# A GpSimd hand in the second output projection: who makes one weight remainder of fourteen

## The chip, the cores and the metric

The kernel runs on one core of a Trainium2 chip. The metric is the device time of one execution in microseconds (us), the median over several runs. The core has five engines that run side by side, each through its own list of instructions in order: TensorE (PE in the profile) multiplies matrices, VectorE (DVE) and ScalarE (ACT) and GpSimd (POOL) work element by element, SyncE (SP) issues DMA transfers. They wait for each other only at semaphores, which count up and are waited for as "at least n".

## The reference, cut to what matters

```python
def first_block(x, ...):
    for layer in range(2):
        y = retention or latent attention of x        # (512, 2048) gated, times w_out (2048, 1024)
        x = _layer_norm(DEEPNORM_ALPHA * x + y, ln_g[layer], ln_b[layer])
...
def _mla_layer(...):
    ...
    return (o * jax.nn.silu(gate)) @ w_out            # the second output projection
...
h = rmsnorm(x, norm_mix_g)                            # second_block begins with it
```

All arrays are float32. 512 tokens, width 1024. The change concerns the product `(o * silu(gate)) @ w_out` of the second layer: (512 x 2048) by (2048 x 1024).

## The kernel before, in words

**Split operands.** A float32 operand is used as two parts: `hi` is a copy that is rounded to the type fp32r (ScalarE makes it), `lo` is what the rounding took away, operand minus `hi` (called the remainder; VectorE or GpSimd makes it with one subtraction, whose two inputs both lie in SBUF). A product takes three matmuls, hi x hi, lo x hi and hi x lo (lines 614 to 616).

**Seven products.** The three output projections AO, BO and DN save an eighth of the multiplications with seven block products in place of eight. In BO each block product `f` (0 to 6) takes two weight panels, so the stage runs over 14 panels, `d` from 0 to 13. A panel is 128 x 2048 floats and goes through five hands:

- SP loads it into one of three stages (`seven_load`, L672); the load of panel `d` waits until the remainder of panel `d - 3` is made, since it lands in the same stage (semaphore `d_tlo`, which counts two halves of every panel).
- ACT rounds the operand (`operand_hi`, semaphore `d_shi`), but only when PE has done the product of panel `d - 3` (`d_pe`), and then the two halves of the panel (`weights_hi`, semaphore `d_thi`). Both are instructions of line 1616.
- DVE makes the operand's remainder (`operand_lo`), the two halves of the panel's remainder (`remainders`, both on L2286) and between the halves the operand of the next panel (`combine`, L2299 to L2305).
- PE multiplies: 24 matmuls a panel, `seven(BO, d, (0, 1))`; the first half of the panel is needed at its first matmul, the second at its thirteenth.
- DVE also adds finished block products into the residual `xres` (`gathers(BO, 1, d)`, lines 2345 to 2378), ahead of `remainders(BO, d)`.

GpSimd makes the remainder of panel 0 (`weights_lo(BO, 0)`) and then has nothing to do until the input weights of the next layer (`split_lo(L0 + 2)`, L793).

**Behind the stage** VectorE goes straight on to the layer norm and the RMS norm of four token tiles (`norms`, lines 2444 to 2471), whose results PE transposes (L996) and multiplies by the next weights. The first instruction of it, L2444, waits for the product of panel 11.

The order on each engine is the order in which the code is written; nothing reorders it. Tile names: `br_hi`, `br_lo`, `s_hi`, `s_lo` are the operand parts (three in turn), `whi`, `wlo`, `whi_a`, `wlo_a` the panel parts, `bT` the input, `comb` combined inputs, `bx` kept block products.

Of the kernel before, what the change touches and what calls it, by code (L numbers as in the profile page):

```python
# [76 lines left out]
BO = Seven(2, 14, 14, END + 8, 8, (36, 36, 36, 36), ((2, 3), (4, 5), (6, 7), (0, 1), (2, 3), (4, 5), (6, 7)))  # L77
UPN, UA = 16, 28
DN = Seven(4, UA + 2 * UPN, 28, END + 16, 16, (36, 36, 36, 40), ((0, 1), (2, 3), (4, 5), (6, 7), (0, 1), (2, 3), (4, 5)))
PANELS = DN.w + 16  # L80
GATHERS, COPIES = 16, 4
HALF = SEQ // 2


# [51 lines left out]
def program(nc, t, out):  # L136
    with ExitStack() as ctx:
        def sb(name, shape, dt=F32, where=ctx):
            return where.enter_context(nc.sbuf_tensor(name, shape, dt))

        def gap(name, lines, where=ctx):
            if lines:
                sb(name, [P, 16 * lines], F32, where)

        def sem(name):
            return ctx.enter_context(nc.semaphore(name))
# [17 lines left out]
        with ExitStack() as h:  # L164
            vs_a = sb("vs_a", [P, 2, 2, PK, HALF], F32R, h)
        gap("gap_a", 256)
        with ExitStack() as h:
            s_hi2 = sb("s_hi2", [P, PK, HALF], F32R, h)
            s_lo2 = sb("s_lo2", [P, PK, HALF], F32R, h)
            comb = sb("comb", [P, KF // 2, HALF], F32, h)  # L170
            stage2 = sb("stage2", [P, PAN], F32, h)
        xhi = sb("xhi", [P, KX, SEQ], F32R)
        xlo = sb("xlo", [P, KX, SEQ], F32R)
        with ExitStack() as h:
            vs_b = sb("vs_b", [P, 2, 2, PK, HALF], F32R, h)
        xres = sb("xres", [P, TT, DM])
# [26 lines left out]
        with ExitStack() as h:  # L203
            gap("gap_ar", 1, h)
            ar_hi = sb("ar_hi", [P, 2, PK, HALF], F32R, h)
            ar_lo = sb("ar_lo", [P, 2, PK, HALF], F32R, h)
# [242 lines left out]
        d_tlo = sem("d_tlo")  # L449
# [29 lines left out]
        def first_half(st, g):  # L479

            x, k = source(st), PK * g
            return x[:, k:k + PK, 0:HALF], x[:, k:k + PK, HALF:]

        def second_half(st, g):

            x, k = source(st), PK * (st.dq + g)
            return x[:, k:k + PK, 0:HALF], x[:, k:k + PK, HALF:]

        def combined(g):

            return comb[:, PK * g:PK * g + PK, :]

        def operand(st, d):

            f, g = divmod(d, st.dq)
            return (first_half(st, g)[0], combined(g), first_half(st, g)[1], combined(g), second_half(st, g)[0],
                    combined(g), second_half(st, g)[1])[f]

        def operand_parts(st, d):

            hi, lo = (ar_hi, ar_lo) if st is AO else (br_hi, br_lo) if st is BO else (dr_hi, dr_lo)
            return (hi[:, d % 3], lo[:, d % 3]) if d % 3 < 2 else (s_hi2[:, :, :], s_lo2[:, :, :])
# [10 lines left out]
        def seven_stage(st, d):  # L513

            if st is DN:
                return up_set(d + 2)[0]
            i = own_panel(st) % 2
            return (stage[i], stage[1 - i], stage2)[d % 3]

        def seven_parts(st, d):  # L520

            if st is DN:
                hi, lo = up_set(d + 2)[1:]
            else:
                hi, lo = ((whi[0], wlo[0]), (whi[1], wlo[1]), (whi_a, wlo_a))[d % 3]
            return hi[:, 0:PAN], lo[:, 0:PAN]
# [259 lines left out]
        def _(pool):  # L786
# [16 lines left out]
            def sum_step(st, i, copies, base):  # L803

                k, g = divmod(i, st.dq)
                if k == 0:
                    add_to_sum(st, 0, g, block_panel(st, 2, g), copies[0], 0)
                elif k == 1:
                    add_to_sum(st, 2, g, block_panel(st, 3, g), copies[0], 0)
                elif k == 2:  # L810
                    add_to_sum(st, 1, g, sum_panel(st, 0, g), copies[1], base + i)
                else:
                    add_to_sum(st, 3, g, sum_panel(st, 1, g), copies[1], base + i)
# [7 lines left out]
            def weights_lo(st, d):  # L821

                hi, lo = seven_parts(st, d)
                for b in range(2):
                    r = slice(b * PAN // 2, (b + 1) * PAN // 2)
                    pool.wait_ge(d_thi, 2 * (st.at + d) + b + 1)
                    pool.tensor_tensor(lo[:, r], seven_stage(st, d)[:, r], hi[:, r].bitcast(F32), ALU.subtract
                                       ).then_inc(d_tlo, 1)
# [45 lines left out]
            for m in range(3 * PAIRS):  # L874
# [7 lines left out]
                elif 11 <= m < 23:  # L882
                    sum_step(DN, m - 11, (36, 44), 24)
            weights_lo(BO, 0)
            pool.wait_ge(w_lo, 2 * (L0 + 2))
            for p in range(L0 + 2, L0 + 6):
                split_lo(p)
# [52 lines left out]
        def _(pe):  # L940
# [48 lines left out]
            def nothing(_):  # L989
                pass  # L990
# [1291 lines left out]
        def _(dve):  # L2282
            own = Own(dve, dv)

            def lo_of(dst, src, hi, signal):
                dve.tensor_tensor(dst, src, hi.bitcast(F32), ALU.subtract).then_inc(signal, 1)  # L2286
# [5 lines left out]
            def combine(st, d):  # L2292

                f, g = divmod(d, st.dq)
                a11, a21 = first_half(st, g)
                a12, a22 = second_half(st, g)
                x = combined(g)
                if f == 1:
                    ins = dve.tensor_tensor(x, a11, a21, ALU.subtract)  # L2299
                elif f == 2:  # L2300
                    ins = dve.tensor_tensor(a21, a22, a21, ALU.subtract)
                elif f == 3:
                    ins = dve.tensor_tensor(x, x, a22, ALU.add)
                elif f == 5:
                    ins = dve.tensor_tensor(x, x, a12, ALU.subtract)  # L2305
                else:
                    return
                ins.then_inc(d_sum, 1)

            def operand_lo(st, d):  # L2310

                hi, lo = operand_parts(st, d)
                dve.wait_ge(d_shi, st.op + d + 1)
                lo_of(lo, operand(st, d), hi, d_slo)

            def weights_lo(st, d):

                dve.wait_ge(d_tlo, 2 * (st.at + d))
                hi, lo = seven_parts(st, d)
                for b in range(2):  # L2320
                    r = slice(b * PAN // 2, (b + 1) * PAN // 2)
                    dve.wait_ge(d_thi, 2 * (st.at + d) + b + 1)
                    lo_of(lo[:, r], seven_stage(st, d)[:, r], hi[:, r], d_tlo)

            def remainders(st, d):

                operand_lo(st, d)
                for b in range(2):
                    r = slice(b * PAN // 2, (b + 1) * PAN // 2)
                    dve.wait_ge(d_thi, 2 * (st.at + d) + b + 1)  # L2330
                    lo_of(seven_parts(st, d)[1][:, r], seven_stage(st, d)[:, r], seven_parts(st, d)[0][:, r], d_tlo)
                    if b == 0 and d + 1 < 7 * st.dq:
                        combine(st, d + 1)
# [482 lines left out]
            for d in range(2, 13):  # L2816
                if d == 4:
                    dve.wait_ge(a_ot, 4 * HA)
                    dve.wait_ge(aux["x"], 16)
                gathers(AO, 0, d)  # L2820
                remainders(AO, d)
            remainders(AO, 13)
            gathers(AO, 0, 13)
            dve.wait_ge(aux["rows"], 16)
# [140 lines left out]
            for d in range(2, 13):  # L2965
                gathers(BO, 1, d)
                if d in (3, 4):
                    dve.wait_ge(bld[d - 1], 32)
                remainders(BO, d)
# [337 lines left out]
```

## Time and profile before

| what | value |
|---|---|
| median of 3 runs | 1385.35 us (1384.39 to 1385.92) |
| profiled execution, its own time | 1385.62 us |
| its span (first to last instruction) | 1383.6 us |
| TensorE busy in the span | 1369.0 us (99%) |
| VectorE, ScalarE, GpSimd busy | 1010.6, 745.4, 305.9 us |
| second output projection (PE) | about 813 to 890 us in the span |

The profile's busy shares are averages over the whole span. For a change in one stage the timeline matters: for each instruction its start, its length, its engine, its line, what it writes and reads, and in brackets how long the engine was idle before it and what ended that. A length is longer than the distance to the next start where instructions of one engine overlap a little. "x2" merges two alike.

### The profile page before, as it was taken

What the parts mean: (1) busy time and instruction counts of PE and PEld (TensorE: products, weight loads), DVE (VectorE), ACT (ScalarE), POOL (GpSimd) and SP (SyncE); (2) the same over time, 40 slices, a digit from 0 to 9 for tenths busy, and PEclk for the clock granted to TensorE, in tenths of its full rate; (3) what the DMA queues carried; (4) which work ended last, traced back from release to release, by engine and by line L of the source; (5) the groups of instructions that cost most, each with busy time, mean ns of one, the idle gap of its engine ahead of it and who ended that gap; (6) DMA issues with size and microseconds to landing.
All of it is one profiled execution on the core that took longest, in us unless ns stands there. A gap on an engine that the chain in (4) does not pass through costs nothing.

```text
span 1383.6 us, 19145 instructions
## 1 busy us (share of the span) xinstructions
PE 1369.0 (99%) x7316; PEld 1183.0 (86%) x7316; DVE 1010.6 (73%) x1667; ACT 745.4 (54%) x1197; POOL 305.9 (22%) x161
## 2 busy tenths in 40 slices
PE   9999999999999999999999999999999999999998
PEld 7888888888888888888888888878888999998887
DVE  7979687889933755554545479936868887889895
ACT  5453635466544443344344356658956566576554
POOL 2050514110134444333433210025213000000000
PEclk9999999999999999999999999999999999999999
DMA  7458565485368988966796557354122675445552
GB/s 268 173 169 237 196 200 174 140 285 197 139 189 216 311 214 233 286 184 153 222 284 180 160 214 270 144 185 134 46 84 77 180 209 150 146 178 213 192 191 103
DMA packets 53898, 260.37 MB, mean 188 GB/s; under 512 B 5568, under 2 KB 10304, under 8 KB 28224
## 3 DMA queue, kind: packets, MB, share of 16 engines
q1 hardware_dynamic: 37152, 163.04, 33.9%
q0 software_dynamic: 5760, 41.95, 15.4%
q10 hardware_dynamic: 10912, 54.40, 11.0%
q8 instruction: 46, 0.75, 0.2%
q14 instruction: 28, 0.23, 0.0%
HBM read 252.03 MB, written 91.23 MB: 248 GB/s over the span
## 4 chain that ended last, share of the span: by engine, by line
PE 80%; DVE 14%; DMA 2%; ACT 2%; issue 1%; POOL 0%; SPq 0%; DVEq 0%; ACTq 0%; POOLq 0%
PE bank L614 21%; PE bank L616 21%; PE bank L615 21%; PE bank L1331 6%; PE bank L1393 3%; PE bank L1282 3%; DVE wlo L2286 3%; PE bank L1310 1%; DVE wlo_a L2286 1%; DMA v_spill<-v_tok 1%; DVE xres L2348 1%; DVE xlo L2286 1%; DVE ar_lo L2286 1%; DVE xres L2464 1%; DMA stage<-tsum 1%
## 5 line engine op out<-in xcount | busy, mean ns | idle before, releaser
L793 POOL TENSOR_TENSOR wlo<-stage,whi 128x1024 fp32r<-128x1024 f32 (+2 forms) x68 | 169.0, 2510 | 435.9 <-ACT whi L1613 349.5
L1616 ACT ACTIVATE whi<-stage 128x1024 fp32r<-128x1024 f32 (+2 forms) x155 | 148.2, 1002 | 109.5 <-PE bank L616 92.5
L2286 DVE TENSOR_TENSOR wlo<-stage,whi 128x1024 fp32r<-128x1024 f32 (+1 forms) x133 | 153.1, 1181 | 12.9 <-ACT whi L1616 12.9
L614 PE MATMUL bank<-xhi,whi 128*128 128x256 f32 (+1 forms) x300 | 98.7, 329 | 1.6 <-POOL wlo L929 1.2
L616 PE MATMUL bank<-xhi,wlo 128*128 128x256 f32 (+1 forms) x300 | 98.5, 328 | 0.0
L615 PE MATMUL bank<-xlo,whi 128*128 128x256 f32 (+1 forms) x300 | 98.4, 328 | 0.0
L1613 ACT ACTIVATE whi<-stage 128x1024 fp32r<-128x1024 f32 (+2 forms) x74 | 76.1, 1079 | 19.2 <-issue 14.2
L2286 DVE TENSOR_TENSOR wlo_a<-stage,whi_a 128x1024 fp32r<-128x1024 f32 (+1 forms) x60 | 71.7, 1220 | 15.2 <-ACT whi_a L1616 15.2
L614 PE MATMUL bank<-whi,xhi 128*128 128x512 f32 (+1 forms) x204 | 78.2, 383 | 0.9 <-POOL wlo L793 0.6
L616 PE MATMUL bank<-whi,xlo 128*128 128x512 f32 (+1 forms) x204 | 77.3, 379 | 0.0
L615 PE MATMUL bank<-wlo,xhi 128*128 128x512 f32 (+1 forms) x204 | 77.2, 378 | 0.0
L1616 ACT ACTIVATE whi_a<-stage 128x1024 fp32r<-128x1024 f32 (+1 forms) x56 | 53.8, 1009 | 19.6 <-PE bank L616 13.9
L614 PEld LDWEIGHTS bank<-xhi,whi 128*128 128x128 f32 x300 | 57.0, 190 | 7.1 <-DVE hid L2496 1.4
L615 PEld LDWEIGHTS bank<-xlo,whi 128*128 128x128 f32 x300 | 57.0, 190 | 5.0
L616 PEld LDWEIGHTS bank<-xhi,wlo 128*128 128x128 f32 x300 | 57.0, 190 | 5.0
L1616 ACT ACTIVATE whi<-oT 128x1024 fp32r<-128x1024 f32 x34 | 34.1, 1053 | 38.2 <-DVE oT L2740 17.9
L842 POOL TENSOR_TENSOR wlo<-stage,whi 128x1024 fp32r<-128x1024 f32 x12 | 30.2, 2532 | 107.6 <-ACT whi L1616 107.6
L2286 DVE TENSOR_TENSOR pt_lo<-bank,pt_hi 128x384 fp32r<-128x384 f32 (+1 forms) x48 | 26.6, 597 | 35.3 <-ACT pt_hi L1616 35.3
L1331 PE MATMUL bank<-xhi,whi 128*128 128x512 f32 x128 | 50.7, 396 | 0.0
L1331 PE MATMUL bank<-xhi,wlo 128*128 128x512 f32 x128 | 50.0, 391 | 0.0
L1331 PE MATMUL bank<-xlo,whi 128*128 128x512 f32 x128 | 49.9, 390 | 0.0
L614 PE MATMUL bank<-ql_hi,whi 128*128 128x512 f32 x120 | 46.9, 391 | 0.0
(493 smaller groups left out, 4341.3 us busy)
## 6 DMA issues: line engine op xcount, KB each, us to landing
stage<-in_w SPq DMA_DIRECT2D x71, 1024.0 KB, 5.0
tsum<-in_w ACTq DMA_DIRECT2D x32, 1024.0 KB, 12.3
stage<-tsum SPq DMA_DIRECT2D x32, 1024.0 KB, 4.8
tsum<-in_w POOLq DMA_DIRECT2D x16, 1024.0 KB, 10.0
tsum<-tsum POOLq DMA_DIRECT2D x16, 1024.0 KB, 10.2
stage<-in_w SPq DMA_DIRECT2D x8, 1152.0 KB, 6.3
usum<-in_w POOLq DMA_DIRECT2D x8, 1024.0 KB, 10.2
stage<-usum SPq DMA_DIRECT2D x32, 256.0 KB, 4.0
```

Of the source, the lines that this page charges most:

```text
L614: pe.matmul(dst, a_hi, b_hi, start=start, stop=False, skip_group_check=onto)
L615: pe.matmul(dst, a_hi, b_lo, start=False, stop=False, skip_group_check=onto)
L616: return pe.matmul(dst, a_lo, b_hi, start=False, stop=stop, skip_group_check=onto)
L793: pool.tensor_tensor(lo[:, r], stage[p % 2][:, r], hi[:, r].bitcast(F32), ALU.subtract).then_inc(w_lo, 1)
L842: pool.tensor_tensor(lo[:, r], a_staged(h, j)[:, r], hi[:, r].bitcast(F32), ALU.subtract).then_inc(g_plo, 1)
L1282: last = pe.matmul(bank[4 + q][:, 0:w], left, right, start=i == 0, stop=i == 4)
L1310: last = pe.transpose(dst[min(kt, 2)][:, at:at + P], prob[:, src:src + P], ident[:, :])
L1331: last = pe.matmul(bank[0][:, :], left[:, k, f], right[:, k, :], start=i == 0, stop=i == 23)
L1393: last = pe.matmul(bank[m][:, :], left[:, k, m * P:(m + 1) * P], right[:, k, :], start=i == 0, stop=i == 23)
L1613: act.activation(parts(p)[0][:, r], stage[p % 2][:, r], ACT.Copy).then_inc(w_hi, 1)
L1616: act.activation(dst, src, ACT.Copy, scale=scale).then_inc(signal, 1)
L2286: dve.tensor_tensor(dst, src, hi.bitcast(F32), ALU.subtract).then_inc(signal, 1)
```

## The change

Panel 10 (the eleventh) of the second output projection gets its remainder from GpSimd. GpSimd runs `weights_lo(BO, 10)` behind `weights_lo(BO, 0)`, with a wait for the remainders of all panels before it, because `d_tlo` counts panels in order. VectorE leaves the two subtractions of panel 10 out and keeps the `combine` that stood between them. Ahead of its first half of panel 11 it waits until GpSimd is done with panel 10, for the same count.

```diff
+BY_GPSIMD = 10
...
             weights_lo(BO, 0)
+            pool.wait_ge(d_tlo, 2 * (BO.at + BY_GPSIMD))
+            weights_lo(BO, BY_GPSIMD)
             pool.wait_ge(w_lo, 2 * (L0 + 2))
...
             def remainders(st, d):
                 operand_lo(st, d)
+                if st is BO and d == BY_GPSIMD:
+                    combine(st, d + 1)
+                    return
+                if st is BO and d == BY_GPSIMD + 1:
+                    dve.wait_ge(d_tlo, 2 * (st.at + d))
                 for b in range(2):
```

On VectorE, from the operand remainder of panel 10 to the panel remainder of panel 11, in the kernel before:

```order
L2286 TENSOR_TENSOR br_lo<-comb,br_hi 128x1024 [waits d_shi]
L2286 TENSOR_TENSOR wlo<-stage,whi 128x1024 [waits d_thi]
L2305 TENSOR_TENSOR comb<-comb,bT 128x1024
L2286 TENSOR_TENSOR wlo<-stage,whi 128x1024 [waits d_thi]
L2348 SCALAR_TENSOR_TENSOR xres<-xres,bx 128x512 [waits d_ev]
L2348 SCALAR_TENSOR_TENSOR xres<-xres,bx 128x512
L2378 TENSOR_TENSOR bx<-bx 128x512 x2
L2286 TENSOR_TENSOR s_lo<-comb,s_hi 128x1024 [waits d_shi]
L2286 TENSOR_TENSOR wlo_a<-stage,whi_a 128x1024 [waits d_thi] x2
```

The same stretch of VectorE in the changed kernel (its line numbers are 3 to 8 higher):

```order
L2289 TENSOR_TENSOR br_lo<-comb,br_hi 128x1024 [waits d_shi]
L2308 TENSOR_TENSOR comb<-comb,bT 128x1024
L2356 SCALAR_TENSOR_TENSOR xres<-xres,bx 128x512 [waits d_ev]
L2356 SCALAR_TENSOR_TENSOR xres<-xres,bx 128x512
L2386 TENSOR_TENSOR bx<-bx 128x512 x2
L2289 TENSOR_TENSOR s_lo<-comb,s_hi 128x1024 [waits d_shi]
L2289 TENSOR_TENSOR wlo_a<-stage,whi_a 128x1024 [waits d_thi,d_tlo]
L2289 TENSOR_TENSOR wlo_a<-stage,whi_a 128x1024 [waits d_thi]
```

The two `wlo` rows of panel 10 are gone, and the first half of panel 11 (`wlo_a`) waits for `d_tlo` too.

On GpSimd, from the end of the attention stage on, before:

```order
L801 DMA tsum<-tsum 128x2048 [waits t_sum,first3]
L793 TENSOR_TENSOR wlo<-stage,whi 128x1024 [waits w_hi] x2
L827 TENSOR_TENSOR wlo<-stage,whi 128x1024 [waits d_thi] x2
L793 TENSOR_TENSOR wlo<-stage,whi 128x1024 [waits w_hi,w_lo]
L793 TENSOR_TENSOR wlo<-stage,whi 128x1024 [waits w_hi] x7
```

And in the changed kernel:

```order
L802 DMA tsum<-tsum 128x2048 [waits t_sum,first3]
L794 TENSOR_TENSOR wlo<-stage,whi 128x1024 [waits w_hi] x2
L828 TENSOR_TENSOR wlo<-stage,whi 128x1024 [waits d_thi] x2
L828 TENSOR_TENSOR wlo<-stage,whi 128x1024 [waits d_thi,d_tlo]
L828 TENSOR_TENSOR wlo<-stage,whi 128x1024 [waits d_thi]
L794 TENSOR_TENSOR wlo<-stage,whi 128x1024 [waits w_hi,w_lo]
L794 TENSOR_TENSOR wlo<-stage,whi 128x1024 [waits w_hi] x7
```

Two subtractions of 128 x 1024 came in behind panel 0's; the other engines' lists are the same.

## Rows read from the trace of the kernel before

**Rows 1.** The page: the span, and the first engine's busy time.
```profile
span 1383.6 us, 19145 instructions
...
PE 1369.0 (99%) x7316; PEld 1183.0 (86%) x7316; DVE 1010.6 (73%) x1667; ACT 745.4 (54%) x1197; POOL 305.9 (22%) x161
```
**Rows 2.** Busy time by stretch: its length, PE, PEld, DVE, ACT, POOL, clock, DMA.
```profile
863.00:878.70 15.70, 15.70 (x71) 12.97 (x71) 15.70 (x22) 9.71 (x11) 0.00 (x0) 1.00 0.33 113
878.70:906.50 27.80, 25.28 (x121) 19.93 (x119) 26.34 (x43) 17.82 (x32) 0.00 (x0) 1.00 0.35 126
906.50:1383.60 477.10, 469.23 (x2832) 418.87 (x2832) 368.92 (x566) 299.08 (x485) 60.00 (x31) 1.00 0.47 151
```
**Rows 3.** Timeline of VectorE around panel 10: start, length, engine, line, tiles, shape.
```profile
858.50 1.23 DVE L2286 TENSOR_TENSOR br_lo<-comb,br_hi 128x1024 fp32r<-128x1024 f32 x1
859.63 1.23 DVE L2286 TENSOR_TENSOR wlo<-stage,whi 128x1024 fp32r<-128x1024 f32 x1
...
861.90 1.23 DVE L2286 TENSOR_TENSOR wlo<-stage,whi 128x1024 fp32r<-128x1024 f32 x1
863.04 1.30 DVE L2348 SCALAR_TENSOR_TENSOR xres<-xres,bx 128x512 f32<-128x512 f32 x2
...
865.45 1.23 DVE L2286 TENSOR_TENSOR s_lo<-comb,s_hi 128x1024 fp32r<-128x1024 f32 x1
866.58 2.36 DVE L2286 TENSOR_TENSOR wlo_a<-stage,whi_a 128x1024 fp32r<-128x1024 f32 x2
...
876.43 2.37 DVE L2286 TENSOR_TENSOR wlo<-stage,whi 128x1024 fp32r<-128x1024 f32 x2
878.76 0.69 DVE L2444 SCALAR_TENSOR_TENSOR xres<-xres,bank 128x512 f32<-128x512 f32 x1
```
**Rows 4.** Timeline of ScalarE: panel 10, operand 11, operand and panel 13.
```profile
857.87 1.99 ACT L1616 ACTIVATE whi<-stage 128x1024 fp32r<-128x1024 f32 x2
862.35 1.06 ACT L1616 ACTIVATE s_hi<-comb 128x1024 fp32r<-128x1024 f32 x1 [2.48 <-PE bank L616]
...
873.23 1.07 ACT L1616 ACTIVATE br_hi<-bT 128x1024 fp32r<-128x1024 f32 x1 [2.48 <-PE bank L616]
874.20 1.99 ACT L1616 ACTIVATE whi<-stage 128x1024 fp32r<-128x1024 f32 x2
```
**Rows 5.** Timeline of TensorE: panel 10's first and thirteenth matmul, panel 11's last.
```profile
867.59 0.39 PE L614 MATMUL bank<-whi,br_hi 128*128 128x512 f32 x1
...
870.31 0.39 PE L614 MATMUL bank<-whi,br_hi 128*128 128x512 f32 x1
...
878.24 0.39 PE L616 MATMUL bank<-whi_a,s_lo 128*128 128x512 f32 x1
```
**Rows 6.** Timeline of TensorE: its wait at the end of VectorE's norm work.
```profile
906.50 0.50 PE L614 MATMUL bank<-whi_a,xhi 128*128 128x512 f32 x1 [0.70 <-DVE xlo L2286]
```
**Rows 7.** Timeline of GpSimd: BO's panel 0, and two halves at 1037 us.
```profile
795.73 4.77 POOL L827 TENSOR_TENSOR wlo<-stage,whi 128x1024 fp32r<-128x1024 f32 x2 [9.91 <-ACT whi L1616]
...
1037.42 2.41 POOL L793 TENSOR_TENSOR wlo<-stage,whi 128x1024 fp32r<-128x1024 f32 x1 [0.68 <-ACT whi L1613]
1039.78 3.38 POOL L793 TENSOR_TENSOR wlo<-stage,whi 128x1024 fp32r<-128x1024 f32 x1
```
**Rows 8.** Timeline of VectorE: two instructions that met a GpSimd subtraction.
```profile
378.50 3.42 DVE L2455 SCALAR_TENSOR_TENSOR oT<-xres,small,rows 128x1024 f32<-128x1024 f32 x1
...
1040.83 3.41 DVE L2286 TENSOR_TENSOR wlo_a<-stage,whi_a 128x1024 fp32r<-128x1024 f32 x1
```
**Rows 9.** Timeline at 33 us: VectorE's instruction, and GpSimd's beside it.
```profile
33.61 1.22 DVE L2286 TENSOR_TENSOR vs_a<-gate,vs_a 128x1024 fp32r<-128x1024 f32 x1
...
32.94 4.17 POOL L850 TENSOR_TENSOR vs_b<-gate,vs_b 128x1024 fp32r<-128x1024 f32 x1 [19.43 <-ACT vs_b L1616]
```
**Rows 10.** SyncE's issue of panel 13's load; the page's time to landing.
```profile
863.16 0.33 SPq L672 DMA_DIRECT2D stage<-tsum  x1
...
stage<-tsum SPq DMA_DIRECT2D x32, 1024.0 KB, 4.8
```

## The prediction

> **What bounds the kernel now.** The page says that TensorE is busy for 1369.0 of 1383.6 us [rows 1], so only 14.6 us of the span can be anybody's waiting, and the question is whether the change touches a place where TensorE waits. I read the busy time by stretch next. From 863 to 878.7 us, inside the second output projection, TensorE is busy for all of 15.70 us, and so is VectorE [rows 2]: two full engines, one beside the other. From 878.7 to 906.5 us TensorE is busy for 25.28 of 27.80 us, so it waits for 2.5 us there [rows 2], and the timeline names VectorE as what ended such a wait: 0.70 us before the matmul at 906.50 [rows 6]. From there to the end TensorE is without work for 7.9 us of 477 by that view [rows 2], so it is the pace again. So TensorE sets the pace up to panel 13, then VectorE's norm work does until 906.5 us, then TensorE again. Whatever moves VectorE's start into the norms, at 878.76 [rows 3], moves the end of the kernel by as much.
>
> Does VectorE come to 878.76 late by itself, or does something hold it there? The last subtractions of the stage start at 876.43 and are followed at 878.76 by L2444 [rows 3], with the same spacing as elsewhere; VectorE isn't idle there. But L2444 needs the product of panel 11, whose last matmul starts at 878.24 and takes 0.39 [rows 5], so it ends at 878.63. VectorE could start the norms only 0.13 us sooner even if it had nothing else to do. And ScalarE paces the panels by TensorE: its operand copies of panels 11 and 13 begin after 2.48 us of idleness that a matmul ended [rows 4]. VectorE's lead over TensorE in the stage can't grow; its delay can.
>
> **The change, step by step.**
>
> Removed from VectorE: two subtractions of 128 x 1024. From 861.90 to the next start at 863.04 is 1.14 us, from 858.50 to 859.63 for the same shape 1.13 [rows 3]. Together -2.28 us of VectorE's list. Taken alone, they would bring VectorE to the operand remainder of panel 11 at 865.45 - 2.28 = 863.17, where the rounded operand is ready only at 862.35 + 1.06 = 863.41 [rows 3, 4]; and at panel 13 the second half of the rounded weights is ready at 874.20 + 1.99 = 876.19, so the last subtraction ends about 1.2 us later, at 877.4, and L2444 then waits for 878.63. So of 2.28 us only 0.13 would come out.
>
> Added to GpSimd: two subtractions of the same shape, 4.77 us for both where nothing disturbs them [rows 7]. GpSimd has no instruction from 800.5 us on until the next layer's weights, and its busy time in the stretches up to 906.5 is 0.00 [rows 2], so nothing is queued behind them that is late. The first half of panel 10 is rounded at 857.87 + 1.05, about 858.9 [rows 4]. Undisturbed, GpSimd is done at 863.7; TensorE wants the first half at 867.59 and the second at 870.31 [rows 5]. Hidden, with 6.6 us to spare for the second half.
>
> Added waits: GpSimd's for the remainder of panel 9 is over before the rounded half is there (VectorE went on to other work before 858.50 [rows 3]). VectorE's, ahead of panel 11's first half, is free if GpSimd is done by then. The load of panel 13 waits for panel 10's remainder: it was issued at 863.16 and such a load lands in 4.8 us [rows 10]; ScalarE wants it at 874.20 [rows 4], so it may be issued 6 us later at no cost.
>
> What the subtractions cost VectorE: here the trace has a warning. At 1040.83 a subtraction of 128 x 1024 on VectorE takes 3.41 us in place of 1.23, and beside it GpSimd's subtraction from 1039.78 takes 3.38 in place of 2.41 [rows 7, 8]. At 378.50 an instruction of the norms with two SBUF inputs takes 3.42 [rows 8] where 1.23 is the length of a subtraction of that size [rows 3]. They take turns: GpSimd waits for one of VectorE's instructions to end, then VectorE's next one waits until GpSimd's is through. The price for VectorE is 3.41 - 1.23 = 2.18 us for each half that GpSimd makes while VectorE's list is full of instructions with two SBUF inputs. From 858.50 to 868.8 it is full of nothing else, since `br_lo`, `comb`, `xres`, `bx`, `s_lo` and `wlo_a` all come from SBUF, and there is no gap in it [rows 3]. Two halves make 2 x 2.18 = +4.36 us.
>
> The Trainium skill says the same of it: SBUF — State Buffer, section "Who interferes with whom", has VectorE and GpSimd share a pair of ports that is locked for a whole instruction, and counts a `tensor_tensor` with both inputs in SBUF among what collides with a GpSimd instruction that reads SBUF. By that rule with the trace's 2.41 us a half, an estimate, VectorE would lose 4.8 us and the change would cost 2.5; the trace's own number is a little lower since the blocked instruction starts up meanwhile.
>
> Bounds of this cost: below 0, if VectorE always keeps its turn (at 33.61 VectorE's instruction took its normal 1.22 us although GpSimd had been waiting since 32.94 and took 4.17 [rows 9]); above, what the second rival gives. I take 2.18 a half, from the row whose shape, tiles and dense neighbours are these.
>
> The sum: -2.28 + 4.36 = +2.08 us at 878.76. Is it taken up by a gap? Before panel 11 the gap that the removal would open (0.24 us, above) doesn't open. Behind it ScalarE's copies are ready earlier than VectorE wants them. TensorE goes on to panel 12 at about 878.5 [rows 5], and its remainder would be ready at 875.3 + 2.1 = 877.4 (the remainder ends about where `br_lo` of panel 13 starts, 1.13 us before 876.43 [rows 3]); panel 13 later still. In the norms VectorE is busy for 26.34 of 27.80 us [rows 2], its few gaps wait for ScalarE's square roots of VectorE's own results and move along. So +2.1 us arrives at 906.5, where TensorE waits for VectorE [rows 6], and from there at the end. Profiled time 1385.62 + 2.1 = 1387.7; that execution lies 0.27 us above the median of the three runs, so the median becomes 1385.35 + 2.1 = **1387.4 us**, 0.15% more. A difference under 0.2% (2.8 us) is about what a measurement of this kernel can't tell from no change, so this forecast falls under "same", if close to its edge.
>
> **The rivals.**
>
> *No collision.* GpSimd works beside VectorE as if alone. Then 0.13 us is gained: 1385.2. Against it are the long rows [rows 8]; for it only that VectorE was undisturbed once [rows 9].
>
> *The whole 2.28 us comes out*: 1383.1. It needs VectorE's list to be the only limit up to 878.76; the 2.48 us waits of ScalarE for TensorE [rows 4] and the end of panel 11 at 878.63 [rows 5] speak against it.
>
> *GpSimd is passed over until VectorE stops* (the other side). If the pattern of 33 us holds, GpSimd doesn't get in between VectorE's instructions; VectorE goes through to the operand remainder of panel 11, starting at 863.45 and ending at 864.7, and stops at its new wait. Only then do both halves run, 4.77 us [rows 7], and panel 11's remainder starts at 869.5 in place of 866.58 [rows 3]: +2.9 us, 1388.2, over 0.2%. This decides as soon as neither half gets in before 864.7. If the first half uses the small gap at 863.2, it is +2.4. TensorE still isn't late: the second half is there at 869.5, wanted at 870.31 [rows 5]. For it speaks one place, against it the turns at 1039 us.
>
> *Something later gives it back.* TensorE's waits behind 906.5 are few, and I know of none that doesn't move along; 1386.
>
> **How the numbers follow.** Turns taken and passed on, +1.6 to +2.7: 0.67. Passed over, +2.4 to +3.2: 0.17. No collision, within half a us of before: 0.09. Given back in part: 0.04. Whole gain: 0.03. The three runs before spread over 1.5 us, so a median of the same kernel can be off by some 0.5 us; the likeliest case's own range is 1386.7 to 1388.2. The overall range reaches down to the no-collision case and up into the passed-over one: 1385.2 to 1388.5. Slower by over 0.2% (above 1388.1): two thirds of "passed over" and a seventh of the likeliest case by scatter, 0.21. Faster by over 0.2%: 0.03. The rest, 0.76, within.
>
> **What would show it.** In the changed kernel's timeline VectorE should have one or two instructions of about 3.4 us between 859 and 868 us, GpSimd two of 2.4 to 3.5 us there, and L2444's counterpart should start near 880.9. The first wait of TensorE in the norms should be about 2 us longer, and the span 1385.7. If VectorE shows normal lengths and an idle stretch before `wlo_a` of panel 11, GpSimd was passed over. If L2444's counterpart starts at 878.7, there was no collision. I would be wrong altogether if TensorE waited inside the stage, which needs another 1.2 us of delay at panel 12, or if a later stage took the shift in.

## The result: 0.13% slower, and the profile after

Side by side on one chip the kernel before took 1386.28 us (median of 22 runs, 1384.39 to 1387.81) and the changed kernel 1387.97 us (22 runs, 1386.85 to 1389.43). The ratio of the two is 1.0013, with a 95% interval of 1.0007 to 1.0019, so the change costs 1.8 us (1.0 to 2.6). That is less than 0.2%, the bound under which the prediction speaks of no change, and the interval holds the +2.1 us of the prediction; with 22 runs of each it can still be told from zero.

The page of the changed kernel has these lines beside [rows 1]: the span is 2.4 us longer, TensorE's work hardly differs, GpSimd has 9.6 us more and VectorE 2.8 us less. (VectorE's 2.8 us are not the work that it was spared: 2.1 of them lie ahead of the stage, where its instructions are the same, and a second execution of the changed kernel shows 1012.5 us for it, more than before.)

```profile
span 1386.0 us, 19147 instructions
...
PE 1369.3 (99%) x7316; PEld 1182.8 (85%) x7316; DVE 1007.8 (73%) x1665; ACT 745.5 (54%) x1197; POOL 315.5 (23%) x163
```

9.6 us for two GpSimd instructions that take 4.77 us where nothing disturbs them [rows 7] is the first sign that something did. The timeline of VectorE after, in place of [rows 3] (start, length, then the instruction, and in brackets the idle time before it and what ended that):

```profile
858.66 1.21 DVE L2289 TENSOR_TENSOR br_lo<-comb,br_hi 128x1024 fp32r<-128x1024 f32 x1
859.80 1.21 DVE L2308 TENSOR_TENSOR comb<-comb,bT 128x1024 f32<-128x1024 f32 x1
860.94 1.28 DVE L2356 SCALAR_TENSOR_TENSOR xres<-xres,bx 128x512 f32<-128x512 f32 x2
862.14 1.28 DVE L2386 TENSOR_TENSOR bx<-bx 128x512 f32<-128x512 f32 x2
863.78 3.00 DVE L2289 TENSOR_TENSOR s_lo<-comb,s_hi 128x1024 fp32r<-128x1024 f32 x1 [0.36 <-ACT s_hi L1619]
869.07 2.36 DVE L2289 TENSOR_TENSOR wlo_a<-stage,whi_a 128x1024 fp32r<-128x1024 f32 x2 [2.29 <-POOL wlo L828]
...
881.20 0.68 DVE L2452 SCALAR_TENSOR_TENSOR xres<-xres,bank 128x512 f32<-128x512 f32 x1
```

And GpSimd's two halves in the same stretch:

```profile
859.39 6.30 POOL L828 TENSOR_TENSOR wlo<-stage,whi 128x1024 fp32r<-128x1024 f32 x1 [58.57 <-ACT whi L1619]
...
865.65 3.38 POOL L828 TENSOR_TENSOR wlo<-stage,whi 128x1024 fp32r<-128x1024 f32 x1
```

GpSimd's first half starts at 859.39, while `br_lo` runs, but `comb` and the four instructions behind it run at their usual lengths and spacing. GpSimd was passed over by five VectorE instructions. At 863.42 VectorE runs out of work for 0.36 us, GpSimd gets in, and now `s_lo` is held up (3.00 us where [rows 3] has 1.23). Then `wlo_a` stands at the wait that the change added, until the second half is done: 2.29 us. That is not the picture that the forecast drew (two VectorE instructions of about 3.4 us and no stop), but the mixed form of its third rival, whose first half uses the small gap.

To compare executions I count from the stage's own start, its first matmul, since the stages before shift whole timelines by a few tenths of a us. It stands in the trace of before and of after at:

```profile
813.12 0.44 PE L614 MATMUL bank<-whi,br_hi 128*128 128x512 f32 x1
```

```profile
813.46 0.44 PE L615 MATMUL bank<-whi,br_hi 128*128 128x512 f32 x1
```

The norms' first instruction starts 878.76 - 813.12 = 65.64 us behind it before [rows 3] and 881.20 - 813.46 = 67.74 us after: +2.10. TensorE's waits between there and 909 us after; of the four, before has the third (1.63 us) and the last [rows 6]:

```profile
888.34 1.09 PE L999 MATMUL bank<-ident,h_tok 128*128 128x128 f32 x8 [1.21 <-DVE h_tok L2479]
892.66 0.50 PE L615 MATMUL bank<-whi_a,xhi 128*128 128x512 f32 x1 [0.48 <-DVE xlo L2289]
905.71 1.09 PE L999 MATMUL bank<-ident,h_tok 128*128 128x128 f32 x8 [1.62 <-DVE h_tok L2479]
908.90 0.50 PE L615 MATMUL bank<-whi_a,xhi 128*128 128x512 f32 x1 [0.70 <-DVE xlo L2289]
```

The delay came out as 1.21 and 0.48 us of new waits for VectorE's norm work. The matmul of the last row stood at 93.38 us in before (906.50 - 813.12) and stands at 95.44 now: +2.06. The view by stretch says the same (length, then TensorE's busy time): TensorE is without work for 29.86 - 25.61 = 4.25 us in the stretch that answers to the second one of [rows 2], where it had 2.52; the other 0.3 us of the 2.06 stand as busy time.

```profile
879.04:908.90 29.86, 25.61 (x120) 19.84 (x118) 28.39 (x44) 17.81 (x32) 0.00 (x0) 1.00 0.37 138
```

Behind it nothing is given back: the stretches to the end are 477.10 us before [rows 2] and 1386.0 - 908.9 = 477.1 us after.

### The profile page after: what moved, and what is told of

Same layout as the page of the kernel before. It is cut to its first block, busy times and chain, and to the rows that moved or that the text cites. A ratio compares the mean times of both kernels' runs of the same rounds, so it can differ in the third digit from the quotient of the medians.

```text
span 1386.0 us, 19147 instructions
## 1 busy us (share of the span) xinstructions
PE 1369.3 (99%) x7316; PEld 1182.8 (85%) x7316; DVE 1007.8 (73%) x1665; ACT 745.5 (54%) x1197; POOL 315.5 (23%) x163
## 4 chain that ended last, share of the span: by engine, by line
PE 83%; DVE 11%; ACT 2%; DMA 1%; issue 1%; POOL 1%; SPq 0%; DVEq 0%; ACTq 0%; POOLq 0%
PE bank L615 22%; PE bank L617 22%; PE bank L616 22%; PE bank L1334 6%; PE bank L1396 3%; PE bank L1285 3%; DVE wlo L2289 2%; PE bank L1313 1%; DVE wlo_a L2289 1%; DVE xlo L2289 1%; DMA v_spill<-v_tok 1%; POOL wlo L828 1%; DVE ar_lo L2289 1%; DVE xres L2472 1%; PE bank L1476 1%
## 5 line engine op out<-in xcount | busy, mean ns | idle before, releaser
L2289 DVE TENSOR_TENSOR wlo<-stage,whi 128x1024 fp32r<-128x1024 f32 (+1 forms) x131 | 150.3, 1176 | 12.7 <-ACT whi L1619 12.7
```

## The experiments

My theory: VectorE and GpSimd can't run instructions with SBUF inputs of this kind at the same time, each GpSimd half takes about 2.2 us from VectorE, and the two outweigh the 2.28 us that VectorE is spared (a relief of which TensorE's pace would let next to nothing through if it came alone). Rivals: the new wait of VectorE is the cost; the cost belongs to this place in the stage; the removal is worth something by itself. Further down it is asked who gets in first. In the diffs a line with `-` is of the changed kernel, one with `+` of the experiment, unless said otherwise; `...` stands for lines left out. The medians are of 11 runs (6 for "GpSimd's work alone") beside 27 or 28 of the kernel before, unless one execution is named. Their intervals are 2.5 to 3.3 us wide, so differences of under 1 us are read from the places in the traces, of one execution each.

**The removal alone.** GpSimd makes only 8 columns of each half of panel 10's remainder, so the other 2032 of 2048 are left out.

```diff
-            weights_lo(BO, BY_GPSIMD)
+            hi, lo = seven_parts(BO, BY_GPSIMD)
+            for b in range(2):
+                r = slice(b * PAN // 2, b * PAN // 2 + 8)
+                pool.wait_ge(d_thi, 2 * (BO.at + BY_GPSIMD) + b + 1)
+                pool.tensor_tensor(lo[:, r], seven_stage(BO, BY_GPSIMD)[:, r], hi[:, r].bitcast(F32), ALU.subtract
+                                   ).then_inc(d_tlo, 1)
```

> GpSimd subtracts 8 columns of each half of panel 10 in place of 1024, VectorE none: 2032 of 2048 columns of that panel's remainder are left as they were, so the product is not the reference's. It is the change without GpSimd's work and so without a collision. Theory (VectorE's lead in the stage is capped by TensorE, the price is the collision): VectorE's 2.28 us come out, but the norms still wait for panel 11's product: 0.1 us faster than before (0 to 0.4), the first norm instruction 0.13 us earlier, and 1.9 us faster than the change. Rival (VectorE's list is the limit of the stage): 2.3 us faster than before.

Measured: 1386.05 us beside 1385.88, ratio 1.0001 (0.9992 to 1.0011). The timeline of VectorE:

```profile
864.05 1.23 DVE L2294 TENSOR_TENSOR s_lo<-comb,s_hi 128x1024 fp32r<-128x1024 f32 x1 [0.36 <-ACT s_hi L1624]
...
874.93 1.23 DVE L2294 TENSOR_TENSOR br_lo<-bT,br_hi 128x1024 fp32r<-128x1024 f32 x1 [0.94 <-ACT br_hi L1624]
...
879.38 0.69 DVE L2457 SCALAR_TENSOR_TENSOR xres<-xres,bank 128x512 f32<-128x512 f32 x1 [0.95 <-PE bank L617]
```

And the last matmul of panel 11 on TensorE:

```profile
878.85 0.39 PE L617 MATMUL bank<-whi_a,s_lo 128*128 128x512 f32 x1
```

The 2.28 us that VectorE is spared are all there, as 0.36 + 0.94 + 0.95 = 2.25 us of new waits, the first two for ScalarE's copies, which TensorE paces, the last for TensorE itself. The norms begin at the same place as before, 65.64 us behind the stage's first matmul. Alone, the removal is worth nothing, and the prediction's 0.13 us wasn't there either: here panel 11's last matmul ends at 878.85 + 0.39 = 879.24 and L2457 starts at 879.38, 0.14 us behind it, though VectorE has been waiting for it. The 0.13 us between 878.63 and 878.76 in the trace of before was such a distance, and not room.

**GpSimd's work alone.** The kernel before, with all its subtractions on VectorE; GpSimd computes panel 10's remainder too, into an idle tile that nobody reads. This diff is against before.

```diff
             for d in range(4, 14):
+                if d == 13:
+                    sp.wait_ge(x_sem, 2)
                 seven_load(BO, d)
...
             weights_lo(BO, 0)
+            hi = seven_parts(BO, 10)[0]
+            to = xlo[:, 0:4, :].rearrange("p k n -> p (k n)")
+            for b in range(2):
+                r = slice(b * PAN // 2, (b + 1) * PAN // 2)
+                pool.wait_ge(d_thi, 2 * (BO.at + 10) + b + 1)
+                pool.tensor_tensor(to[:, r], seven_stage(BO, 10)[:, r], hi[:, r].bitcast(F32), ALU.subtract
+                                   ).then_inc(x_sem, 1)
...
+                        if round_ == 2 and q == 0 and c == 0:
+                            dve.wait_ge(x_sem, 2)
```

> The kernel before, in which VectorE keeps all its work, and GpSimd subtracts panel 10 as well, into a tile that is free then. It is the price of the collision alone. Theory (port shared, each half of GpSimd's holds up one VectorE instruction of two SBUF inputs by 1.8 to 2.2 us): 3.6 to 4.4 us slower than before. If GpSimd takes turns with VectorE's dense list, the two long VectorE instructions lie between 859 and 866 us; if it is passed over until the list has a gap or an instruction that reads PSUM, they lie behind 869 us. Rival (the cost of the change is its new wait, not the port): no change.

Measured: 1389.95 us beside 1385.88, ratio 1.0028 (1.0016 to 1.0040), +3.9 us. VectorE and GpSimd in its timeline:

```profile
858.63 1.22 DVE L2296 TENSOR_TENSOR br_lo<-comb,br_hi 128x1024 fp32r<-128x1024 f32 x1
859.77 3.42 DVE L2296 TENSOR_TENSOR wlo<-stage,whi 128x1024 fp32r<-128x1024 f32 x1
863.11 3.41 DVE L2315 TENSOR_TENSOR comb<-comb,bT 128x1024 f32<-128x1024 f32 x1
866.44 1.21 DVE L2296 TENSOR_TENSOR wlo<-stage,whi 128x1024 fp32r<-128x1024 f32 x1
...
859.32 6.11 POOL L893 TENSOR_TENSOR xlo<-stage,whi 128x1024 fp32r<-128x1024 f32 x2 [58.49 <-ACT whi L1626]
```

Here are the forecast's turns: two instructions of 3.4 us in a row, 2.2 us more each, and the norms 69.79 us behind the first matmul, +4.15. No instruction on VectorE waits for GpSimd's result in this stage, so a wait isn't needed for the cost.

**The changed kernel without VectorE's wait.** A semaphore of its own tells TensorE and SyncE that GpSimd's halves are done, and VectorE no longer stops for them; GpSimd's own wait for the panels before goes too. All subtractions are made.

```diff
-            pool.wait_ge(d_tlo, 2 * (BO.at + BY_GPSIMD))
-            weights_lo(BO, BY_GPSIMD)
+            hi, lo = seven_parts(BO, BY_GPSIMD)
+            for b in range(2):
+                r = slice(b * PAN // 2, (b + 1) * PAN // 2)
+                pool.wait_ge(d_thi, 2 * (BO.at + BY_GPSIMD) + b + 1)
+                pool.tensor_tensor(lo[:, r], seven_stage(BO, BY_GPSIMD)[:, r], hi[:, r].bitcast(F32), ALU.subtract
+                                   ).then_inc(x_sem, 1)
             pool.wait_ge(w_lo, 2 * (L0 + 2))
+            pool.sem_inc(d_tlo, 2)
...
-                        pe.wait_ge(d_tlo, 2 * (st.at + d) + kk // 2 + 1)
+                        if st is BO and d == BY_GPSIMD:
+                            pe.wait_ge(x_sem, kk // 2 + 1)
+                        else:
+                            pe.wait_ge(d_tlo, 2 * (st.at + d) + kk // 2 + 1 - (2 if st is BO and d > BY_GPSIMD else 0))
...
-                if st is BO and d == BY_GPSIMD + 1:
-                    dve.wait_ge(d_tlo, 2 * (st.at + d))
```

> The change with a semaphore of its own for panel 10's remainder, so that VectorE doesn't stop ahead of panel 11 (TensorE and the load of panel 13 wait for it instead). Theory (port): VectorE no longer shows a wait for GpSimd, but a subtraction of panel 11 takes about 3.4 us in its place; 1.5 to 2.2 us slower than before, as the change. Rival (the new wait is the cost): the 2.3 us stop goes away and the time is within 0.4 us of before.

Measured: 1387.76 us beside 1385.88, ratio 1.0019 (1.0010 to 1.0028). Its VectorE:

```profile
859.34 3.42 DVE L2319 TENSOR_TENSOR comb<-comb,bT 128x1024 f32<-128x1024 f32 x1
862.69 3.49 DVE L2365 SCALAR_TENSOR_TENSOR xres<-xres,bx 128x512 f32<-128x512 f32 x2
```

The second row holds two instructions, the first of which took 2.89 us by itself. No stop is left, and the norms still begin 1.90 us later (67.54). The wait is a place where the cost can show, not its cause; without it the loss sits in the instructions. The two terms of the sum can now be told apart: beside GpSimd's work VectorE's relief is worth 4.15 - 1.90 = 2.25 us, nearly all of its 2.28, although it is worth nothing alone.

**One half instead of two.** VectorE makes the first half of panel 10 and GpSimd the second.

```diff
-            pool.wait_ge(d_tlo, 2 * (BO.at + BY_GPSIMD))
-            weights_lo(BO, BY_GPSIMD)
+            hi, lo = seven_parts(BO, BY_GPSIMD)
+            r = slice(PAN // 2, PAN)
+            pool.wait_ge(d_tlo, 2 * (BO.at + BY_GPSIMD) + 1)
+            pool.wait_ge(d_thi, 2 * (BO.at + BY_GPSIMD) + 2)
+            pool.tensor_tensor(lo[:, r], seven_stage(BO, BY_GPSIMD)[:, r], hi[:, r].bitcast(F32), ALU.subtract
+                               ).then_inc(d_tlo, 1)
...
+                    r = slice(0, PAN // 2)
+                    dve.wait_ge(d_thi, 2 * (st.at + d) + 1)
+                    lo_of(seven_parts(st, d)[1][:, r], seven_stage(st, d)[:, r], seven_parts(st, d)[0][:, r], d_tlo)
                     combine(st, d + 1)
                     return
```

> GpSimd makes the second half of panel 10 alone, VectorE the first. Theory: VectorE saves 1.14 us and is held up once by 2.2 (turns) or stops until GpSimd is through (passed over, since its list has no gap now): 1.0 to 1.3 us slower than before. Rival (the wait for GpSimd's second half is the cost, whatever the first does): as the change, 1.8 to 2.1 us slower.

Measured: 1386.83 us beside 1385.88, ratio 1.0007 (0.9998 to 1.0016); norms at 66.63, +0.99, half of the change's +2.10. The interval alone allows both no cost and the change's; by the place in the trace the cost goes with the number of halves. Its timeline, VectorE's last rows before the wait and GpSimd's one half:

```profile
864.31 1.22 DVE L2293 TENSOR_TENSOR s_lo<-comb,s_hi 128x1024 fp32r<-128x1024 f32 x1
867.82 2.36 DVE L2293 TENSOR_TENSOR wlo_a<-stage,whi_a 128x1024 fp32r<-128x1024 f32 x2 [2.29 <-POOL wlo L890]
...
860.93 6.85 POOL L890 TENSOR_TENSOR wlo<-stage,whi 128x1024 fp32r<-128x1024 f32 x1 [60.23 <-DVE wlo L2293]
```

This is the third rival undiluted: GpSimd comes at 860.93 and isn't let in until VectorE stops at 865.53; 2.29 us later it is done. So one half costs 2.29 us as a stop, where it costs 2.2 as a long instruction.

**Panel 3 or panel 13 instead of panel 10.** The two edits are `BY_GPSIMD = 3` and `BY_GPSIMD = 13`.

> The change with panel 3 in place of panel 10, the whole edit otherwise the same. There VectorE stood idle for 1.44 us before panel 4, whose load was late, so it has room. Theory (port): two halves cost 2 x 2.18 us less the 2.28 that VectorE saves, less up to 1.44 us of idleness: 0.4 to 1.0 us slower than before. Rival (the cost is fixed to the hand-over, wherever it is): as the change, 1.8 to 2.1 us slower.

> The change with the last panel, 13, in place of 10. VectorE stops for no remainder behind it and goes to the norms, where the first instruction waits for TensorE and reads PSUM. Theory (port): GpSimd's first half meets VectorE's idle time and the PSUM reading instruction, only its second half holds up one instruction of the norms, for up to 1.5 us: 1.0 to 1.6 us slower than before, with no wait of VectorE for GpSimd. Rival (the cost is the new wait of VectorE): no slower than before.

Measured for panel 3: 1386.36 us beside 1385.68, ratio 1.0003 (0.9994 to 1.0013), norms +0.35. For panel 13: 1386.43 us, ratio 1.0006 (0.9997 to 1.0015), norms +0.00, but TensorE's matmul of [rows 6] +0.57. VectorE around panel 3 in the kernel before, then with panel 3 handed over, then with panel 13 (and GpSimd's second half there):

```profile
830.63 1.23 DVE L2286 TENSOR_TENSOR wlo<-stage,whi 128x1024 fp32r<-128x1024 f32 x1 [1.44 <-ACT whi L1616]
```

```profile
825.49 3.43 DVE L2304 TENSOR_TENSOR bT<-bT 128x1024 f32<-128x1024 f32 x1
830.17 2.09 DVE L2289 TENSOR_TENSOR br_lo<-bT,br_hi 128x1024 fp32r<-128x1024 f32 x1 [1.26 <-ACT br_hi L1619]
```

```profile
878.49 0.69 DVE L2452 SCALAR_TENSOR_TENSOR xres<-xres,bank 128x512 f32<-128x512 f32 x1 [2.44 <-PE bank L617]
...
879.47 2.28 DVE L2463 SCALAR_TENSOR_TENSOR h_tok<-xres,small,rows 128x1024 f32<-128x1024 f32 x1
...
878.26 2.40 POOL L828 TENSOR_TENSOR wlo<-stage,whi 128x1024 fp32r<-128x1024 f32 x1
```

The turns are taken wherever both engines are at it: 3.43 for 1.22 at panel 3, 2.28 for 1.28 in the norms. What they cost in the end is a matter of place. Behind panel 3 VectorE stood idle for 1.44 us anyway, and with the change it comes to that subtraction of panel 4 (832.18, the first matmul being at 814.25) only 0.42 us later than before. At panel 13 the second half runs into the norms and takes 1.00 us from `h_tok`, of which 0.57 is left at TensorE, less than the 1.0 to 1.6 us that I expected. Both intervals hold zero, so it is the traces that show these costs. Note the 0.69 at 878.49: it lies beside GpSimd's second half (878.26 to 880.66) and keeps its length; one of its inputs comes from the accumulators (`bank`), not from SBUF.

**Who gets in first?** The changed kernel showed GpSimd passed over by five instructions in a row, while the runs without VectorE's wait showed it let in at once. One difference was that in the changed kernel GpSimd's subtraction carries two waits. Three single executions look at that: the run without VectorE's stop, with the second wait put back on GpSimd's first half; the changed kernel again, as it is; and the changed kernel with a tiny GpSimd instruction ahead that carries the wait.

```diff
             weights_lo(BO, 0)
             pool.wait_ge(d_tlo, 2 * (BO.at + BY_GPSIMD))
+            pool.memset(small[:, 3, 7:8], 0.0)
             weights_lo(BO, BY_GPSIMD)
```

> The kernel in which VectorE doesn't stop, with the change's second wait on GpSimd's first subtraction (for the remainder of panel 9, long made by then). It asks who gets the port first. In the changed kernel GpSimd's first half was passed over by five VectorE instructions, without the stop and this wait it got in at the next one. If the second wait makes the difference, GpSimd's first half takes over 4 us here, until VectorE's list has its first gap; if the small difference in time did, or VectorE's stop, it takes about 2.8 us.

> The changed kernel once more, unaltered, for one look, to see whether who gets in between is settled by the program or varies from one execution to the next. If it is settled by the program (the instructions ahead leave GpSimd in the same place each time): GpSimd's first half again waits through five VectorE instructions and shows 6.3 us, s_lo 3.0 us. If it hangs on a small difference of times: GpSimd's first half may show 2.7 us with comb at 3.4 us, and VectorE's stop of 2.3 us before wlo_a goes. The cost is near 2 us in either case, 1387.5 to 1388.2.

> The changed kernel with one very small GpSimd instruction (a zero written into one unused number of each partition) ahead of panel 10's first half, so that it and not the subtraction carries the wait for the remainders of panels 0 to 9; the subtraction then waits for ScalarE alone. If the double wait of the subtraction is why it was passed over: comb 3.4 us, GpSimd's halves 2.7 and 3.4 us. If not: s_lo 3.0 us and 6.3 us as in the changed kernel. Time within 0.3 us of the changed kernel's in either case, 1387.5 to 1388.2.

Measured, one execution each: 1387.61 (before 1385.68), 1388.92 (before 1386.91) and 1388.18 us (before 1386.91, too). In all three GpSimd was let in behind `br_lo`, in the unaltered kernel too; its second execution has these rows on VectorE, and on GpSimd:

```profile
859.14 1.22 DVE L2289 TENSOR_TENSOR br_lo<-comb,br_hi 128x1024 fp32r<-128x1024 f32 x1
860.27 3.42 DVE L2308 TENSOR_TENSOR comb<-comb,bT 128x1024 f32<-128x1024 f32 x1
863.62 3.49 DVE L2356 SCALAR_TENSOR_TENSOR xres<-xres,bx 128x512 f32<-128x512 f32 x2
867.03 1.28 DVE L2386 TENSOR_TENSOR bx<-bx 128x512 f32<-128x512 f32 x2
868.23 1.21 DVE L2289 TENSOR_TENSOR s_lo<-comb,s_hi 128x1024 fp32r<-128x1024 f32 x1
869.37 2.35 DVE L2289 TENSOR_TENSOR wlo_a<-stage,whi_a 128x1024 fp32r<-128x1024 f32 x2
...
881.49 0.68 DVE L2452 SCALAR_TENSOR_TENSOR xres<-xres,bank 128x512 f32<-128x512 f32 x1
```

```profile
859.89 2.72 POOL L828 TENSOR_TENSOR wlo<-stage,whi 128x1024 fp32r<-128x1024 f32 x1 [58.55 <-ACT whi L1619]
...
862.57 3.38 POOL L828 TENSOR_TENSOR wlo<-stage,whi 128x1024 fp32r<-128x1024 f32 x1
```

So the second wait isn't the reason, and the program doesn't settle it: the same kernel shows the one pattern in one execution and the other in the next. GpSimd's start against VectorE's doesn't tell them apart either: 0.73 us behind the start of `br_lo` when it was passed over, 0.75 and 0.69 us when it was let in (this one, and the one with the tiny instruction). Here the stage's first matmul is at 813.96, so the norms begin at 67.53, +1.89. The price hardly depends on the pattern: +2.10 passed over, +1.90 (without VectorE's wait) and three times +1.89 with turns.

**GpSimd where its result would be worth something.** The kernel before, but a remainder that VectorE makes inside the norms, where TensorE does wait for VectorE, goes to GpSimd: input weight panel L0 + 1. The diff is against before.

```diff
             weights_lo(BO, 0)
+            pool.wait_ge(w_lo, 2 * (L0 + 1))
+            split_lo(L0 + 1)
...
-                    panel_lo(panel + 1, 0)
-                    panel_lo(panel + 1, 1)
```

> The kernel before, with another hand-over: GpSimd makes the remainder of the second weight panel behind the stage (L0 + 1), VectorE's two subtractions of it leave the norms, where TensorE waits for VectorE. VectorE's instructions that read PSUM lie beside GpSimd's first half and behind it. Theory (port): VectorE saves 2.27 us, is held up by 1.4 us at the scaling of tile 1 and by about 0.2 at the centring of tile 2: 0.2 to 0.8 us faster than before, unless TensorE then waits for the panel's second half. Rival (each half costs VectorE 2.18 us wherever it is): 2.1 us slower.

Measured: 1385.71 us beside 1385.68, ratio 1.0000 (0.9991 to 1.0009). My expectation of a gain fell. VectorE, GpSimd and TensorE in its timeline:

```profile
892.25 2.84 DVE L2473 SCALAR_TENSOR_TENSOR h_tok<-xres,small,grow 128x1024 f32<-128x1024 f32 x1
895.01 0.67 DVE L2446 SCALAR_TENSOR_TENSOR xres<-xres,bank 128x512 f32<-128x512 f32 x1
...
896.47 1.29 DVE L2288 TENSOR_TENSOR xlo<-bank,xhi 128x512 fp32r<-128x512 f32 x2 [0.52 <-ACT xhi L1618]
...
891.62 5.71 POOL L793 TENSOR_TENSOR wlo<-stage,whi 128x1024 fp32r<-128x1024 f32 x2 [90.91 <-DVE wlo_a L2288]
```

```profile
895.14 1.09 PE L998 MATMUL bank<-ident,h_tok 128*128 128x128 f32 x8 [1.66 <-DVE h_tok L2473]
903.43 1.09 PE L998 MATMUL bank<-ident,h_tok 128*128 128x128 f32 x8 [0.32 <-DVE h_tok L2473]
```

VectorE is spared 2.27 us here too, and `h_tok` gives back 2.84 - 1.28 = 1.56 of it; only one instruction is held up, since the others beside GpSimd read from `bank`. TensorE's waits change places: there is a new one of 1.66 us at 895, and the one at 903 is 0.32 in place of 1.63 us. With a difference of -0.09 us at the matmul of [rows 6] nothing is left. What took the remaining 0.6 us I can only name (0.52 us of VectorE's idleness at 896.47, for a ScalarE copy); no run takes it apart. No kernel tried beat the kernel before.

## Why the prediction was right

**The bound.** TensorE paces the stage, and VectorE's start into the norms moves the end. Shown: +2.10 at the norms became +2.06 at TensorE's matmul behind them; +4.15 became +4.13, +0.99 became +0.98. The form was a little different from the one foretold: not a longer wait of TensorE at one place but, in the changed kernel, two new ones.

**The removal.** The sum had -2.28 for it, against GpSimd's price on the same list, and said that alone only 0.13 of this would come out. Both held in the main: beside GpSimd's work it gave 2.25, alone 0.00. The 0.13 was off: it took the distance between the end of panel 11's product and L2444 for room, but the run without the subtractions shows the same distance where VectorE waits for that product. In the profiled execution of before VectorE reached `br_lo` of panel 10 45.38 us behind the stage's first matmul, in the changed kernel 45.20, and in nine of the ten runs behind it 45.18 or 45.19 (the tenth, panel 3, has other work ahead of it). That execution of before happened to be 0.20 us late there, and used up a slack that is otherwise visible: the last experiment, which has the stage as before, waits 0.18 us for TensorE ahead of its first norm instruction.

**GpSimd's price.** Forecast at 2 x 2.18 = 4.36 us; alone, it gave +4.15 at the norms from two instructions of 3.42 and 3.41 us, which are together 4.4 us longer than usual, less that 0.20 of slack. In the execution with turns the sum reads -2.28 + 2.20 + 2.20 - 0.20 = +1.92, measured +1.89. The 2.18 came from one row [rows 8], and that row was right. That +2.08 was forecast and +2.10 came out in the first profiled execution is luck to the last 0.2 us: the forecast left out the slack, and that execution had the dearer pattern (next). The forecast time, 1387.4 us, can't be set against the measured 1387.97 as it stands: it was counted from 1385.35, the median of three runs, where 22 runs gave 1386.28. What can be compared is the difference, 1.8 us (1.0 to 2.6) where the forecast had 2.1.

**The pattern.** This step of the prediction held in one execution and failed in the other. It said "GpSimd waits for one of VectorE's instructions to end, then VectorE's next one waits until GpSimd's is through", and gave 0.67 to that and 0.17 to being passed over. The first profiled execution shows the latter: 0.44 until `s_lo`, 1.77 in it, 2.38 at the wait (2.29 idle, and the usual overlap of 0.09) make 4.59, less 2.28 is 2.31 from `br_lo` on, and 0.2 of it is the slack. The rival's own price for it was +2.4. The second execution and four experiments at panel 10 show turns; the first and the one with one half show GpSimd passed over. The time was right although the pattern varies, because both come to the same: each half needs its 2.3 us free of VectorE's two-input work, whether that is taken inside an instruction or in a stop.

**Hidden work and loads.** That GpSimd's result would be in time for TensorE held: the second half ended at 869.03, and TensorE shows no wait in the stage. That the later load of panel 13 costs nothing held too: ScalarE's copies of panel 13 kept their place behind 2.48 us of idleness that a matmul ended.

**Given back later.** It isn't, as far as these traces can tell: 477.1 us from the matmul of [rows 6] to the end in both. That they agree so well is chance, since this stretch took 1386.8 - 909.2 = 477.6 us in the second execution of the changed kernel, and 476.4 to 477.8 over all the runs. The medians say the same, with +1.8 us at the end of the kernel.

## What to carry to other kernels

Work that is given to an idle engine isn't free if the two engines lock each other out: here one 128 x 1024 subtraction on GpSimd takes 2.2 us from a busy VectorE, where making it itself costs VectorE 1.14 us, so the hand-over loses about 1 us a half even before anything else. Look in the trace of before for one instruction that met such a neighbour, and price every moved instruction by it; then ask which wait ends last at the place, since the same relief of 2.28 us is worth nothing where TensorE's pace swallows it, and nearly all of itself where VectorE's list is late anyway. So add up relief and delay on the engine's own list first, and compare the sum with the pace of the other engine after that. If GpSimd is to help, its hours are those in which VectorE waits anyway (panel 3 cost 0.35 us at the norms, in one trace, where panel 10 cost 2) or reads from the accumulators.

## What the runs showed of the hardware

- A GpSimd subtraction with its inputs in SBUF that arrives while VectorE runs two-input SBUF instructions back to back is sometimes let in after the one that is running (2.72 to 2.79 us for the first half, five traces) and sometimes passed over by five of them, until VectorE pauses (6.30 and 6.85 us). This differed between two executions of one kernel, with the same instructions around it and starts within 0.02 us of each other. What decides it stays open. The Trainium skill (SBUF — State Buffer, section "Who interferes with whom") states of the pair of ports that the two engines share that it is an exclusive lock, and that issue order decides who blocks. The changed kernel's trace agrees only in part: `s_lo` stood still while GpSimd worked (3.00 us for 1.23), but GpSimd's instruction starts at 859.39, before `comb` at 859.80, and `comb` still went first.
- Where GpSimd's second half followed one that had held up a VectorE instruction, it got in right behind that instruction, in each of the eight traces that have this, and took 3.37 to 3.40 us with its wait; undisturbed it takes about 2.4 (2.41 [rows 7], 2.40 at 878.26).
- The VectorE instructions that were held up all had two SBUF inputs, large or small, `tensor_tensor` or `scalar_tensor_tensor`: a 128 x 512 `xres` of 0.68 us took 2.89 us (at 862.69, without VectorE's wait). Those with an input from `bank` kept their lengths beside GpSimd (0.67 us at 895.01, 0.69 us at 878.49). The same section of the Trainium skill states that a VectorE instruction with at most one SBUF input, outside the two-port modes, doesn't contend with GpSimd; these rows agree.
